# Two-layer diffusion step: an earlier first slot table, filler products on TensorE, fewer vector products

## The reference

```python
mp = ada_params(cond_ctx, mod_w[l], mod_b[l])        # silu(cond) @ mod_w + b, cut in six
hp = modulate(xp, mp[0], mp[1])                      # x * (1 + scale) + shift
# mixer: layer 0 RWKV-7 and convolution, layer 1 differential attention
xp = post_norm(xp, mp[2] * mix_p, ln1_g[l], ln1_b[l])            # layer_norm(alpha * x + y)
xp = post_norm(xp, mp[5] * hier_moe(modulate(xp, mp[3], mp[4]), *moe), ...)
# attention: attn = softmax(q1 k1) - lam * softmax(q2 k2); o = attn @ v;
#            o = o * rsqrt(mean(o * o) + eps) * subln_g * (1 - lam_init), per head
# hier_moe: best of 4 groups, then best 2 of its 8 experts for each token
hid = silu(h @ w_gate[e]) * (h @ w_up[e]);  out = (hid * gate) @ w_down[e]
```

## Time and profile before

| what | value |
|---|---|
| median of three timed runs | 993.96 us |
| profiled execution, its own time | 992.27 us |
| its span in the profile | 990.5 us |
| TensorE busy | 858.1 us (87%) |
| VectorE busy | 493.6 us (50%) |
| ScalarE busy | 190.7 us (19%) |
| granted TensorE clock, mean | 0.915 |
| DMA moved | 226.81 MB, mean 229 GB/s |

### The profile page before, as it was taken

The page is one execution under the profiler, slowest core; times in us unless marked ns, Lnnn a source line. Parts: engine busy times, 40 slices in busy tenths (PEclk is TensorE's granted clock), DMA queues, the critical chain, the costliest instruction groups (busy, mean ns, idle before and its releaser), DMA issues.

```text
span 990.5 us, 14329 instructions
## 1 busy us (share of the span) xinstructions
PE 858.1 (87%) x5132; PEld 520.6 (53%) x5132; DVE 493.6 (50%) x1282; ACT 190.7 (19%) x514; POOL 42.0 (4%) x62
## 2 busy tenths in 40 slices
PE   3799989999999989758898977899879667998894
PEld 1587865777687765453353433344555443543351
DVE  1244688887863775663242326011375652532246
ACT  0125631222211211210010101100541200110010
POOL 1000230000010000000000001000000000000000
PEclk9699999999999989859898978999879778998997
DMA  9921278554454410399959582744000699868971
GB/s 368 416 123 65 85 280 358 201 229 173 175 203 152 187 43 22 111 423 391 398 209 414 216 340 93 304 169 182 31 1 1 261 396 423 342 276 355 395 307 42
DMA packets 29068, 226.81 MB, mean 229 GB/s; under 512 B 4104, under 2 KB 4520, under 8 KB 8032
## 3 DMA queue, kind: packets, MB, share of 16 engines
q1 hardware_dynamic: 25504, 214.57, 54.5%
q0 software_dynamic: 3520, 11.66, 3.5%
HBM read 286.74 MB, written 2.39 MB: 292 GB/s over the span
## 4 chain that ended last, share of the span: by engine, by line
PE 66%; DVE 13%; DMA 12%; SPq 4%; issue 3%; ACT 1%; DVEq 0%; ACTq 0%
DMA arena<-in_w_exp 9%; PE ps L1303 9%; PE ps L901 8%; PE ps L1249 7%; PE ps L1008 5%; PE ps L1221 5%; PE ps L796 4%; PE ps L1277 3%; PE ps L1232 3%; PE ps L847 3%; PE ps L825 3%; DMA arena<-in_mod_w 2%; SPq L654 2%; PE ps L1016 2%; DVE arena L2064 1%
## 5 line engine op out<-in xcount | busy, mean ns | idle before, releaser
L1249 PE MATMUL ps<-arena 128*32 128x512 f32 x960 | 121.7, 659 | 31.3 <-DMA arena<-in_w_exp 29.2
L1249 PEld LDWEIGHTS ps<-arena 128*32 128x32 f32 x960 | 32.4, 119 | 116.1 <-issue 78.6
L1418 ACT ACTIVATE arena<-ps 128x256 f32<-128x256 f32 (+1 forms) x122 | 47.9, 428 | 233.6 <-PE ps L825 137.6
L1303 PE MATMUL ps<-arena 128*128 128x512 f32 x192 | 87.1, 614 | 5.4 <-issue 2.3
L901 PE MATMUL ps<-arena 128*128 128x256 f32 x368 | 83.2, 385 | 1.5 <-ACT arena L1426 1.5
L1221 PEld LDWEIGHTS ps<-arena 128*128 128x128 f32 x544 | 66.1, 202 | 24.4 <-issue 24.4
L825 PE MATMUL ps<-arena 128*128 128x128 f32 x368 | 59.9, 301 | 21.5 <-DVE arena L1805 9.3
L1221 PE MATMUL ps<-arena 128*128 128x128 f32 x544 | 69.2, 288 | 10.5 <-DVE arena L2313 10.5
L901 PEld LDWEIGHTS ps<-arena 128*128 128x128 f32 x368 | 70.2, 192 | 14.7 <-ACT arena L1426 1.9
L2362 DVE TENSOR_SCALAR arena<-arena 128x256 f32<-128x256 f32 x15 | 4.4, 295 | 144.6 <-ACT arena L1635 144.6
L796 PE MATMUL ps<-arena 128*32 128x512 f32 x384 | 53.8, 666 | 19.3 <-DMA arena<-in_cst 12.8
(11 more groups left out here) (329 smaller groups left out, 1072.3 us busy)
## 6 DMA issues: line engine op xcount, KB each, us to landing
arena<-in_w_exp SPq DMA_DIRECT2D x180, 1024.0 KB
arena<-in_mod_w SPq DMA_DIRECT2D x24, 2048.0 KB, 7.6
arena<-in_od_in_w SPq DMA_DIRECT2D x6, 2048.0 KB, 9.8
arena<-in_ev_in_w SPq DMA_DIRECT2D x5, 2048.0 KB, 28.7
arena<-in_ev_out_w SPq DMA_DIRECT2D x2, 2048.0 KB, 7.5
arena<-gate_rows POOLq DMA_DIRECT2D x8, 512.0 KB, 7.8
arena<-in_ln POOLq DMA_DIRECT2D x4, 1024.0 KB, 10.2
arena<-in_od_out_w SPq DMA_DIRECT2D x2, 2048.0 KB, 8.1
```

The lines of the kernel that those rows point to most:

```text
L1249: mm = pe.matmul(ps[32 * c:32 * c + 32, 6, :], xg[:, k, 32 * c:32 * c + 32], EW[:, c, k * 512:(k + 1) * 512], start=(k == 0), stop=(k == K ...
L1303: mm = pe.matmul(BK.bank(key), hT[:, k, s * T:(s + 1) * T], slot(("odin", c))[:, k, :], start=(k == 0), stop=(k == KT - 1))
L1418: BK.drained_by(A(out, take(key)[:, 0:n], ACT.Copy), key)
```

## The change

The diff has these parts. (a) At the start the transposes of x stand ahead of `mod(0, 3)`, in the plan too. (b) A function `warm(n)` issues n products of the identity with itself into bank 7, which nobody reads; it stands at the start, in `moe` and ahead of the transposes between the layers. (c) `BK2` has bank 6 alone; `count` and `pos` become keys of `BK`. (d) In `moe` VectorE works out the slots of step 0 directly from `pos` and the stream-0 table, before the chunk table, and `eid` is made between the two halves of `gather(0)`; the two memsets move ahead of the logits. (e) In attention q is scaled by -1/8 when it is copied, so the reduction takes minima and needs no scaling afterwards. (f) The sums of squares for the head norm move from VectorE to ScalarE (Square with accumulation). In layer 1 a wait for `mix11_read` moves up to the first `warm`.

```diff
-    BK2 = Banks(ps, [6, 7], S("filled_side"), {"dve": S("drained_side")})
+    BK2 = Banks(ps, [6], S("filled_side"), {"dve": S("drained_side")})
...
     for c in range(4):
+        if c == 3:
+            for s in range(NS):
+                for h2 in range(2):
+                    BK.add(("xT", "m0", s, h2), "act" if h2 == 0 else "x0")
         plan_mod(0, c)
         plan_fold(0, c)
...
-        for kind in ("count", "pos", "base", "eid"):
+        for kind in ("count", "pos"):
+            BK.add((kind, l), "dve")
+        for kind in ("base", "eid"):
             BK2.add((kind, l), "dve")
...
+        def warm(n):
+            for _ in range(n):
+                pe.matmul(ps[:, 7, 0:P], ident, ident, start=True, stop=True)
...
-        for c in range(4):
+        for c in range(3):
             mod(0, c)
             fold(0, c)
         pe.wait_ge(S("ld_x"), 32)
         x_transposes("m0")
+        warm(9)
+        mod(0, 3)
+        warm(3)
+        fold(0, 3)
+        warm(7)
         wait_hT("m0")
...
             rows(l, 0)
+            if l == 1:
+                pe.wait_ge(S("mix11_read"), 2)
+            warm(17)
             turn_x(l, 1)
+            warm(6)
             logits(l, 1)
             rows(l, 1)
+            warm(12)
...
-            gather(0)
+            warm(6)
+            gather(0, range(4))
+            side_free("eid")
+            pe.wait_ge(S("ended"), l + 1)
+            pe.matmul(side("eid")[0:1, 0:NC * MAXS], ones[0:32, 0:1], rt_[0:32, R_CMP:R_CMP + NC * MAXS],
+                      start=True, stop=True).then_inc(filled_side, 1)
+            gather(0, range(4, KT))
...
+        warm(24)
         for s in range(NS):
             for h2 in range(2):
                 pe.wait_ge(S("x_part") if h2 == 0 else S("x_new"), s + 1 if h2 == 0 else norm_no(0, 1, s) + 1)
                 sums_free(("xT", "m1", s, h2))
                 transposes(("xT", "m1", s, h2), [x[:, s, (4 * h2 + n) * P:(4 * h2 + n + 1) * P] for n in range(4)])
             sums_free(("qkv", s, 0))
+            warm(5 - 2 * s)
             project_in(s, 0)
...
-                rsqrt(st8[:, 16 + g:20 + g], st8[:, 8 + g:12 + g], "at_var", NORMS[n] + 1, "at_rstd")
+                s = NORMS[n] // 2
+                BK.wait_drained(act, ("pv", s, g // 4))
+                for h in range(4):
+                    o = slice((g + h) * P, (g + h + 1) * P)
+                    ins = A(t1k[:, o], OO[:, s, o], ACT.Square, accum_out=st8[:, 24 + g + h:25 + g + h])
+                    own.inc(ins)
+                own.wait()
+                own.link(A(st8[:, 16 + g:20 + g], st8[:, 24 + g:28 + g], ACT.Ln, scale=1.0 / P, bias=st8[:, 8:9]))
+                A(st8[:, 16 + g:20 + g], st8[:, 16 + g:20 + g], ACT.Exp, scale=-0.5).then_inc(S("at_rstd"), 1)
...
+            inside, first_slot = rv(R_T4, 64, "p (s n) -> p s n", s=NS), rv(R_ZERO, 64, "p (s n) -> p s n", s=NS)
+            own.inc(STT(inside, pos, float(CH), both(rv(R_F, 32)), ALU.is_lt, ALU.mult))
+            own.link(STT(first_slot, pos, 1.0, both(rv(R_RF, 32)), ALU.add, ALU.add))
+            read(V.tensor_copy(slot_of, pos), "pos")
+            own.link(TT(first_slot, first_slot, inside, ALU.mult))
+            place = rt_[:, R_A:R_A + 4]
+            for pick, oh in ((0, P1), (1, P2)):
+                own.link(TT(rv(R_T, 64), oh, rv(R_ZERO, 64), ALU.mult))
+                own.link(V.tensor_reduce(place[:, 2 * pick:2 * pick + 2], rv(R_T, 64, "p (s n) -> p s n", s=NS), AX, ALU.add))
+            own.link(TS(place, place, 1.0, None, ALU.subtract))
+            choose(0, 0, place)
...
-                own.inc(V.tensor_reduce(q[:, 2 * z:2 * z + 2], bank.rearrange("p (m n) -> p m n", m=2)[:, :, 0:nk],
-                                        AX, ALU.max))
-            for z in range(2):
-                own.wait(own.n - 1 + z)
-                sig(TS(q[:, 4 + 2 * z:6 + 2 * z], q[:, 2 * z:2 * z + 2], -HD ** -0.5, None, ALU.mult), "smax")
+                sig(V.tensor_reduce(q[:, 4 + 2 * z:6 + 2 * z], bank.rearrange("p (m n) -> p m n", m=2)[:, :, 0:nk],
+                                    AX, ALU.min), "smin")
```

132 lines of the change are left out of this document (58 added, 74 removed).

## The result

The changed kernel took 982.17 us in the median of four timed runs (980.10 to 984.38); the kernel before took 993.61 in the median of its four (989.53 to 997.06). The ratio is 0.989, 95% interval 0.984 to 0.993. The profiled execution took 983.66 us with a span of 981.8, against 992.27 and 990.5. The prediction, 986.5 with 981.5 to 990.5, had the direction and, within that range, the size; the narrower range of the forecast itself, 983 to 989, was missed by 0.8 us, and not every term of the sum was right, as the stages show.

The account below looks back on a forecast made before the run. TensorE, busy 87% of the span, was held differently in five stretches, with expert loads binding at routing. Terms 3.0 + 1.35 - 0.9 + 3.2 + 0.8 = 7.45 us gave 984.8 profiled, 986.5 timed; range 981.5 to 990.5, forecast itself 983 to 989.

Parts of the forecast that it names:

- Start, 3.0: Start, up to the input projection: transposes moved ahead of the fourth product and fillers save 3.0 us; bounds -1 and +4.5.
- a bad case: Start: transposes and fillers all at half clock end at 32.9, 3 us past the fourth product's weights.
- Rival 1: Start: transposes and early fillers stay at half clock, gain only 0.8 us, total 988.7; chance 0.20.
- Mixture of experts, 1.35 and 0.8: Routing, layers 0 and 1: expert loads bind, so 10 us of faster routing become 1.35 and 0.8 us.
- my 10: Routing: the expert loop starts about 435.5 instead of 445.67, 10 us earlier.
- Norm, -0.9: Norm between layers: bank wait delays transposes, rsqrt, x_new of stream 1 and odin loads; loses 0.9 us, bounds -3 and +2.
- Rival 4: Norm: fillers keep the clock up across 630.50 (+2) or the bank wait costs nothing (+0.9); total 984; chance 0.12.
- Attention, 3.2: Attention: less VectorE work on statistics and scaling brings the out projection 3.2 us earlier; bounds 0.5 and 5.5.
- Rival 2: Attention: ScalarE becomes the bound, aT copies wait behind squares; term only 0.5, total 989.2; chance 0.14.
- Rivals 3 and 5: 3: routing gain passes whole, 2 x 10, 968.7, chance 0.04; 5: fillers never reach full clock, 7.2 slower, chance 0.03.

Follow-up runs that it names:

- in the second: The changed kernel run once more, unchanged, beside new runs of the kernel before: 981.26 us, ratio 0.990 (0.985 to 0.994).

## Why the prediction was right, term by term

The sum was 7.45 us. With the means of the table it is 2.9 (start, up to the mixture of experts) + 2.5 + 0.1 + 2.2 + 0.0 = 7.7, and each term is known to 1 us at best. The timed medians say 11.4 in the first comparison and 7.6 in the second. That 7.45 lies so near 7.7 is in part luck: layer 0 and the norm came out better than their terms, attention and layer 1 worse, by about 1 us each.

- **Start, 3.0.** Right in the mean, 410.45 to 407.52, and in its two parts: 1.2 at the begin of the projection (40.01 to 38.77) and, of the rest, 1.2 in the projection itself, whose 176 instructions took 38.40 in all six profiles of the changed start and 40.01, 38.37 and 40.31 in the three of before. The reason for a bad case was wrong. I let it depend on whether the clock rises during the transposes and fillers; in the first profile the first, second and third product all ran at half clock (3.64, 3.64 and 3.61), ahead of both. Rival 1's value for the start (0.8) came out there, not its mechanism. Its rule from the Trainium skill ("TensorE: Matmul & The Clock Gate", Part 4, PE-mode transpose: transposes do not count as activity) decided nothing here: the transposes ran at full clock behind a product at full clock (1.96 for 16 at 26.72 above) and behind one at half (1.97 at 29.10), and partly at half in others (2.61 at 27.02). In every start they stand beside products, and no run isolates them.
- **Mixture of experts, 1.35 and 0.8.** The mechanism is shown three ways: no loss from slower routing without fillers, none from a delay, 19.0 us in these stages between the kernels with half loads. The size in layer 0 is 2.5 in the mean to the last scatter (186.27 to 183.78). But at the second half of step 1, where the first loads have done their part, it is 1.4 (62.01 to 60.60 after the transposes), which is the term. The other 1.1 come later, behind waits for weights that the change does not touch: 32 instructions after the wait of step 4 took 6.49 and 6.44 in the two profiles of before and 4.96 to 6.60 in the six of after. That is the clock, and with two profiles on one side it is not shown that the change has a part in it. In layer 1 the size is below what differs between executions (240.7 to 243.3 for the same code). The loop started 8.5 us earlier, counted from the transposes, for my 10.
- **Norm, -0.9.** The step was right to the tenth for the bank (transposes 11.43 behind the scatter, forecast 609.7 - 598.28 = 11.4) and the rsqrt stood behind the modulations; the load came 1.4 late by the first pair, 1.0 by the second, for the 0.9. What I priced wrong was the entry into chunk 1. I took the half-clock entry for given, and it is not. It costs 1.7 us when it occurs. It occurred in three of six profiles with the bank of before and no fillers, and in none of five with the late bank and fillers. It did not occur with the late bank and no fillers (one profile, norm 101.28), and it did in one of two with fillers and the bank of before. As far as so few profiles tell, the steadier entry comes with the late bank and not with the fillers, which the prediction rightly took for worthless. In the mean the term is 0.1 (101.31 to 101.25), with 2.7 between the outcomes of the code of before: the loss at the load and the steadier entry cancel. The forecast of -0.9 was a right mechanism and half of the account; the bounds held it. Rival 4 named the other half, at 2 us, but laid it to the fillers.
- **Attention, 3.2.** 2.2 in the mean, with 3.5 in the first pair. What was mis-sized is the part of the minima and of the clock. The prediction has no clock in this term. At equal clock the squares are worth 1.1, the minima 0.4 to 0.5 on the way with nothing of it visible at the end, and the rest, up to 2.3, is the last value products at full clock, which happened in three of eleven profiles. The 3.2 is reached in these three alone; the first profile was one of them, which is luck. Rival 2 (0.5) is excluded: the eleven profiles lie 1.1 to 3.5 below the two of before.
- **Rivals 3 and 5.** The routing's gain passes only when the loads are halved. The fillers reached full clock: the 34 of the routing took 3.96 us in the first profile (411.46), 0.12 each.

## What to carry to other kernels

Two chains that end within 3 us of each other (here the routing and twelve loads) hide each other: shortening the loads brought nothing, the routing about 2 us, both 19 over two layers, and the trace shows it beforehand as a DMA share near 1 up to the moment at which the other ends. Fillers are worth what the products right behind them save, on the path. Ahead of a wait for a transfer they saved nothing here. Inside one they brought the products behind to full clock five times in six, and no total time that shows. Stages of a kernel that keeps crossing between two clocks differ by 1 to 3 us from one execution to the next: compare a stage over several profiles before a term of a sum is called right or wrong.

## What the runs showed of the hardware

- The granted clock of a window and the durations disagree at the start. From 16 to 20 us in the changed kernel the window shows 1.00,

```profile
16.00:20.00 4.00, 2.96 (x16) 0.60 (x16) 0.69 (x1) 0.00 (x0) 0.00 (x0) 1.00 1.00 426
```

  while the 16 instructions took 3.64, what they take at a granted clock of 0.50 and nearly twice their 1.93. Ahead of the first recorded change the durations are the better witness.
- Four values read into TensorE's registers and tested cost it 1.3 to 1.6 us of idle in each step; one value, read ahead of two more waits, cost none that shows. Number and place of the reads changed together, so which of the two did it is open.
- With fillers up to about 13 us, the weights of the fourth product landed at 31.2, 31.0 and 30.8 instead of 29.9, though the loads of the first 9 us, but for the first two, were issued only 0.14 to 0.4 us later. Why was not tried.
